# The RWKV-7 recurrence put on the crossing quadrants of TensorE, and run in common beats with the inversion and the scores

## The reference, cut to what matters

```python
def wkv7(r, w, k, v, a, b):
    # S_t = S_{t-1} diag(w_t) + (S_{t-1} a_t) b_t^T + v_t k_t^T ;  y_t = S_t r_t
    def step(S, inp):
        r_t, w_t, k_t, v_t, a_t, b_t = inp
        sa = jnp.einsum('bhvk,bhk->bhv', S, a_t)
        S = S * w_t[:, :, None, :] + sa[..., None] * b_t[:, :, None, :] + v_t[..., None] * k_t[:, :, None, :]
        y = jnp.einsum('bhvk,bhk->bhv', S, r_t)
        return S, y
```

## Time and profile before

| | us |
|---|---|
| median of 3 executions | 2024.97 |
| the profiled execution's own time | 2027.18 |
| its span, first to last instruction | 2025.4 |
| in it the stage of the change (L2182 to the start of L2347) | 213.5 |

### The profile page before, as it was taken

The page is one execution under the profiler, slowest core; times in us unless marked ns, Lnnn a source line. Parts: engine busy times, 40 slices in busy tenths (PEclk is TensorE's granted clock), DMA queues, the critical chain, the costliest instruction groups (busy, mean ns, idle before and its releaser), DMA issues.

```text
span 2025.4 us, 35146 instructions
## 1 busy us (share of the span) xinstructions
PE 1967.9 (97%) x14308; PEld 1602.1 (79%) x14308; DVE 1158.7 (57%) x1805; ACT 783.1 (39%) x1399; POOL 207.3 (10%) x164
## 2 busy tenths in 40 slices
PE   7999999999999999998999999999999999999997
PEld 3877899877787887775777887877888888888885
DVE  6789666576434444466475747485555256556423
ACT  7767333334222222437532222134243244344211
POOL 2000222200202012004202102020000010000001
PEclk9999999999999999998999999999999989999999
DMA  5320000222333222220244454534531222332421
GB/s 194 138 94 22 3 4 4 86 102 82 102 101 94 93 94 84 90 89 32 91 161 159 153 171 141 191 141 144 171 104 32 65 92 83 106 101 83 148 92 42
DMA packets 61004, 201.48 MB, mean 99 GB/s; under 512 B 8000, under 2 KB 11200, under 8 KB 59584
## 3 DMA queue, kind: packets, MB, share of 16 engines
q1 hardware_dynamic: 60096, 192.93, 28.7%
q10 hardware_dynamic: 768, 6.55, 1.0%
HBM read 190.68 MB, written 6.42 MB: 97 GB/s over the span
## 4 chain that ended last, share of the span: by engine, by line
PE 71%; issue 17%; DVE 7%; ACT 2%; POOL 2%; DMA 0%; DVEq 0%; POOLq 0%; SPq 0%; ACTq 0%
PE bank L2033 17%; PE bank L2035 17%; PE bank L2034 17%; POOL HS L2843 2%; PE bank L2218 1%; PE bank L2250 1%; PE bank L2265 1%; PE bank L2222 1%; DVE GBZ L1435 1%; DVE HR L1618 1%; PE bank L2519 1%; DVE wlo L1251 1%; PE bank L2505 1%; PE bank L2539 1%; PE bank L2682 1%
## 5 line engine op out<-in xcount | busy, mean ns | idle before, releaser
L1251 DVE TENSOR_TENSOR wlo<-raw,whi 128x1024 fp32r<-128x1024 f32 x270 | 327.3, 1222 | 568.9 <-ACT whi L696 566.3
L696 ACT ACTIVATE whi<-raw 128x1024 fp32r<-128x1024 f32 x270 | 282.3, 1057 | 708.6 <-PE bank L2035 695.7
L2033 PE MATMUL bank<-inh,whi 128*128 128x512 f32 x1200 | 470.7, 392 | 1.9 <-DVE inl L1495 1.6
L2035 PE MATMUL bank<-inh,wlo 128*128 128x512 f32 x1200 | 467.1, 389 | 0.0
L2034 PE MATMUL bank<-inl,whi 128*128 128x512 f32 x1200 | 467.0, 389 | 0.0
L2033 PEld LDWEIGHTS bank<-inh,whi 128*128 128x128 f32 x1200 | 225.2, 188 | 58.3 <-issue 6.6
L2035 PEld LDWEIGHTS bank<-inh,wlo 128*128 128x128 f32 x1200 | 225.2, 188 | 47.1
L2034 PEld LDWEIGHTS bank<-inl,whi 128*128 128x128 f32 x1200 | 225.3, 188 | 46.8 <-issue 0.7
L2033 PE MATMUL bank<-hidh,whi 128*128 128x512 f32 x576 | 228.5, 397 | 8.2 <-DVE HR L1618 5.5
L2035 PE MATMUL bank<-hidh,wlo 128*128 128x512 f32 x576 | 224.5, 390 | 0.0
L2034 PE MATMUL bank<-hidl,whi 128*128 128x512 f32 x576 | 224.3, 389 | 0.0
(11 more groups left out here) (423 smaller groups left out, 2853.0 us busy)
## 6 DMA issues: line engine op xcount, KB each, us to landing
raw<-in_mlp_w SPq DMA_DIRECT2D x128, 512.0 KB, 3.6
ADW<-in_w_ada SPq DMA_DIRECT2D x32, 768.0 KB, 5.0
raw<-in_w_up SPq DMA_DIRECT2D x44, 512.0 KB, 3.5
raw<-in_w_in SPq DMA_DIRECT2D x28, 512.0 KB, 3.7
raw<-in_a_w_rkv SPq DMA_DIRECT2D x24, 512.0 KB, 3.5
raw<-in_w_down SPq DMA_DIRECT2D x22, 512.0 KB, 3.5
raw<-in_a_wo SPq DMA_DIRECT2D x8, 512.0 KB, 7.6
raw<-in_b_wq SPq DMA_DIRECT2D x8, 512.0 KB, 3.4
```

The source lines that it names most:

```text
L696: act.activation(whi[u % SLOTS][:, :], raw[u % SLOTS][:, :], ACT.Copy).then_inc(w_hi, 1)
L1251: dve.tensor_tensor(lo[:, :], r[:, :], h[:, :].bitcast(F32), ALU.subtract).then_inc(w_lo, 1)
L2033: pe.matmul(o, w[:, wc], xh, start=start, stop=False)
L2035: return pe.matmul(o, r[:, wc], xh, start=False, stop=stop)
```

## The change

The token space of a head moves to the other partition half. The scores of head h are still read from `head(h)` but are written to `head(1 - h)` (`cross(h)`), which is the quadrant off the diagonal. VT, KT, BT, the masked scores, the inverse, WB and UB of head h so lie on the other half. The state and the channels stay. By this the narrow and wide scores, the product A S (`correction`, bank 4) and the four products into bank 6 (`off`) are crossing matmuls; the inversion and the products into bank 5 (`output_states`, `values_sum`, `solved`) stay on the diagonal.

The three loops are replaced by one over 50 beats. Ten beats make one pair of chunks, two beats (one for each chunk) a level. A beat of TensorE has three slots: the left product of one chunk, interleaved matmul by matmul with `off` of the recurrence or with a narrow score job; the bank 5 products with a narrow score job; the right product of the left product of the beat before, with a wide score job. Then comes `correction`, and in the first eight beats one bonus sum each. The pair in the inversion is g, the recurrence runs on g-1 in steps of two blocks (8 steps in 10 beats), the scores belong to g and g+1. What a job's table does not have for the last pair is left out there. The last ten beats hold the recurrence of the last pair alone.

The recurrence is arranged anew: ScalarE copies the three products of bank 5 at once (128x384); VectorE adds the A S part and the values part into WB, adds the two parts of the output into RT, and makes the new state in two instructions of 128x64; GpSimd multiplies AT and RT of each chunk but the first by the decay FS (`scaled`, two 128x512 instructions), which the state is no longer multiplied by beforehand. ScalarE squares a whole chunk of the output at once. Z and the inverse have two banks (0 and 1) in place of four. GBZ has six buffers in place of four. `early_sums` runs in beat 42, the three early reciprocals in beats 44 to 46. SyncE waits for `off` of step 23 (beat 39) and of step 31 (beat 49).

The number of matmuls does not change: 768 in the scores, 1280 in the inversion, 992 in the recurrence, 8 bonus and 8 early sums, 3056 in all.

```diff
+        GROUPS = NCH // 2
+        PER, RPER = 2 * LEVELS, CB
+        BEATS = PER * GROUPS + RPER + 2
+        MASKED = {0: (0, 3), 1: (0, 4), 2: (2, 0), 4: (2, 1), 5: (1, 3), 7: (1, 4), 8: (3, 0), 9: (3, 1)}
+        COPIED = {0: (0, 5), 1: (2, 2), 3: (0, 6), 4: (0, 7), 6: (1, 5), 7: (3, 2), 8: (1, 6), 9: (1, 7)}
+        AHEAD_OF_TIME = (((0, 0), 2), ((0, 1), 4), ((0, 2), 3), ((1, 0), 6), ((1, 1), 7), ((1, 2), 5))
+        VSUM_AT, VROOT_AT, VINV_AT = PER * GROUPS + 2, PER * GROUPS + 3, (PER * GROUPS + 4, PER * GROUPS + 5, PER * GROUPS + 6)
+
...
+        GBZ = [at(f"GBZ{n}", kb, [CB, P]) for n, kb in enumerate((32, 40, 192, 196, 16, 24))]
...
-            sp.wait_ge(STEP["pe_rec"].sem, STEP["pe_rec"].at(("y", NCH // 2 - 2, 2 * CB - 1)))
+            sp.wait_ge(STEP["pe_rec"].sem, STEP["pe_rec"].at(("off", RPER * (GROUPS - 1) - 1)))
...
+            for beat in range(BEATS + 1):
+                q, u, c, r = inverse_at(beat), recurrence_at(beat - 1), job_at(COPIED, beat), recurrence_at(beat - 3)
+                w2 = recurrence_at(beat + 1)
+                if q:
+                    act.wait_ge(pi.sem, pi.at(("q", *q)))
+                    act.activation(QS[q[2]][:], pairs(PB[q[2]][:]), ACT.Copy).then_inc(ai.sem, ai.step(("q", *q)))
+                if u is not None or w2 is not None:
+                    part = slice(2 * P if u is None else 0, 2 * P if w2 is None else 3 * P)
+                    act.wait_ge(pr.sem, pr.at(("diag", beat)))
+                    act.activation(DIAG[beat % 2][:, part], PB[5][:, part], ACT.Copy).then_inc(ar.sem, ar.step(("diag", beat)))
+                if c:
+                    score_copy(*c, 3)
+                if r is not None and r % (RPER // 2) == RPER // 2 - 1:
+                    j = chunk_of(r)[0]
+                    act.wait_ge(dr.sem, dr.at(("y", r)))
+                    act.activation(KT[:, :, tok(j)], RT[:, :, tok(j)], ACT.Square).then_inc(ar.sem, ar.step(("y", j)))
+                if beat == VROOT_AT:
+                    act.wait_ge(STEP["pe_gn"].sem, STEP["pe_gn"].at("early"))
+                    act.activation(KNI[:, 0:EARLY], PB[0][:, 0:EARLY], ACT.Sqrt, scale=1.0 / HD, bias=small[:, 1:2]).then_inc(ag.sem, ag.step("early root"))
...
+            def states_next(r):
+
+                j, cbs = chunk_of(r)
+                dve.wait_ge(pr.sem, pr.at(("off", r)))
+                if j > 0:
+                    dve.wait_ge(dr.sem, dr.at(("m", r - RPER // 2)))
+                for n in range(2):
+                    cb = cbs.start + n
+                    if j == 0:
+                        mm = dve.tensor_copy(SM[1][:, cb, :], PB[6][:, tok(n)])
+                    else:
+                        mm = dve.scalar_tensor_tensor(SM[(j + 1) % 2][:, cb, :], SM[j % 2][:, cb, :], FS[:, cb, j - 1:j], PB[6][:, tok(n)], ALU.mult, ALU.add)
...
+            for beat in range(BEATS):
+                z, m, w, y = inverse_at(beat - 1), job_at(MASKED, beat), recurrence_at(beat), recurrence_at(beat - 2)
+                if y is not None:
+                    if y < RPER * GROUPS - RPER // 2:
+                        states_next(y)
+                    outputs(y)
+                if z:
+                    inverse_sum(*z)
+                if m:
+                    score_mask(*m, 2)
+                if w is not None:
+                    corrections(w)
+                if beat == 0:
+                    turned(0, 0, 1)
+                if z:
+                    g, lv, x = z
+                    if lv < LEVELS - 1:
+                        turned(g, lv + 1, x)
+                    elif g < GROUPS - 1:
+                        turned(g + 1, 0, x)
+                if beat < CB:
+                    bonus(beat)
+                if beat in VINV_AT:
+                    early_inverse(VINV_AT.index(beat))
             dve.drain().then_inc(phase, 1)
             dve.wait_ge(phase, phase_done("dve"))
             pg, ag = STEP["pe_gn"], STEP["act_gn"]
@@ -2176,171 +2236,215 @@
 
             dsc, atk = STEP["dve_score"], STEP["act_tok"]
             din, ain, drc, arc = STEP["dve_inv"], STEP["act_inv"], STEP["dve_rec"], STEP["act_rec"]
...
+            def score_wide(j, job, bank, a):
+
+                cb = a + 4 * (job % 3)
+                for h in range(2):
+                    hs = head(h)
+                    mm = pe.matmul(PB[bank][cross(h), chunk(a)], (BT if job < 2 else KT)[hs, cb, tok(j)], RA[hs, :, cb, tok(j)], start=True, stop=True)
+                if a == 3:
...
+            def off(r, n):
+
+                j, cbs = chunk_of(r)
+                cb, part = cbs.start + n // 4, n % 4
+                if part < 2 and j < NCH - 1:
+                    for h in range(2):
+                        ts = cross(h)
+                        if part == 0:
+                            pe.matmul(PB[6][head(h), tok(n // 4)], KT[ts, cb, tok(j)], VT[j % 4][ts, cb, :], start=True, stop=False)
                         else:
+                            pe.matmul(PB[6][head(h), tok(n // 4)], BT[ts, cb, tok(j)], UB[(beat_of(r) + 1) % 2][ts, tok(n // 4)], start=False, stop=True)
+                if part >= 2:
+                    for h in range(2):
+                        ts = cross(h)
+                        if part == 2:
+                            mm = pe.matmul(PB[6][head(h), tok(2 + n // 4)], VT[j % 4][ts, cb, :], GKM[j % 4][ts, cb, 0:HC], start=True, stop=False)
                         else:
+                            mm = pe.matmul(PB[6][head(h), tok(2 + n // 4)], UB[(beat_of(r) + 1) % 2][ts, tok(n // 4)], GBZ[j % 6][ts, cb, 0:HC], start=False, stop=True)
+                    if n == 7:
+                        mm.then_inc(pr.sem, pr.step(("off", r)))
...
+                    mm = pe.matmul(PB[5][head(h), tok(n)], GBZ[j % 6][head(h), cb, HC:P], WB[r % 2][head(h), tok(n)], start=True, stop=True)
...
+                for n in range(2):
+                    cb = cbs.start + n
+                    for h in range(2):
+                        mm = pe.matmul(PB[4][cross(h), tok(n)], AT[head(h), cb, tok(j)], SM[j % 2][head(h), cb, :], start=True, stop=True)
+                mm.then_inc(pr.sem, pr.step(("w", r)))
...
+            for beat in range(BEATS):
+                q, z = inverse_at(beat), inverse_at(beat - 1)
+                m, c = job_at(MASKED, beat), job_at(COPIED, beat)
+                w, u, y, w2 = (recurrence_at(beat - ago) for ago in (0, 1, 2, -1))
+                c_at = 0 if y is None else 2 if m is None and z else 1
+                if c and c_at == 0:
+                    score_free(COPIED, beat)
+                if y is not None:
+                    off_ready(y)
+                if q:
+                    inverse_left_ready(*q)
+                for n in range(CB):
+                    if q:
+                        inverse_left(*q, n)
+                    if y is not None:
+                        off(y, n)
+                    elif c and c_at == 0:
+                        score_narrow(*c, 3, n)
+                if c and c_at == 1:
+                    score_free(COPIED, beat)
+                if w2 == 0:
+                    pe.wait_ge(dp.sem, dp.at(("bonus", CB - 1)))
+                elif u is not None or w2 is not None:
+                    pe.wait_ge(arc.sem, arc.at(("diag", beat - 1)))
+                for n in range(CB):
+                    if n in (0, 1) and w2 is not None:
+                        mm = values_sum(w2, n)
+                        if n == 1 and u is None:
+                            mm.then_inc(pr.sem, pr.step(("diag", beat)))
+                    if n in (2, 3) and u is not None:
+                        output_states(u, n - 2)
+                    if n in (4, 6) and u is not None:
+                        mm = solved(u, n // 2 - 2)
+                        if n == 6:
+                            mm.then_inc(pr.sem, pr.step(("diag", beat)))
+                    if c and c_at == 1:
+                        score_narrow(*c, 3, n)
+                if z:
+                    pe.wait_ge(ain.sem, ain.at(("q", *z)))
+                    pe.wait_ge(din.sem, din.at(("t", *z)))
+                if m:
+                    score_free(MASKED, beat)
+                if c and c_at == 2:
+                    score_free(COPIED, beat)
+                for n in range(CB):
+                    if z:
+                        inverse_right(*z, n)
+                    if m and n % 2 == 0:
+                        score_wide(*m, 2, n // 2)
+                    if c and c_at == 2:
+                        score_narrow(*c, 3, n)
+                if w is not None:
+                    correction(w)
+                if beat < CB:
+                    bonus(beat)
+                if beat == VSUM_AT:
+                    early_sums()
...
+            for x in range(2):
+                prepare(x)
+                level_mask(0, 0, x)
+            for g in range(GROUPS):
+                for lv in range(1, LEVELS):
                     for x in range(2):
```

(37 more changed lines are left out.)

406 lines of the change are left out of this document (164 added, 242 removed).

## The result

| | before | after |
|---|---|---|
| median, runs | 2029.27 us, 7 | 2014.70 us, 7 |
| lowest to highest | 2024.61 to 2031.27 | 2010.99 to 2021.21 |
| ratio, 95% interval | | 0.9937 (0.9922 to 0.9952) |
| ratio on a second chip job (6 and 12 runs) | | 0.9936 (0.9924 to 0.9947) |
| the profiled execution: time, span | 2027.18, 2025.4 | 2010.99, 2009.0 |

0.9937 of 2029 us is 12.8 us less (9.7 to 15.8); forecast were 16. The profiled execution of after was the fastest of its seven, so its 16 us are at the upper end; a second trace, of a run of 2017.0 us span, has a stage of 200.9 us. Of the executions behind the experiments, one of 3239.92 us (mean granted clock 0.555; the kernel "both heads, apart") is left out of its ratio, and the trace of "both heads at once" is of its slowest execution, 2235.49 us, where the median is 2204.46.

The account below looks back on a forecast made before the run. TensorE's instruction supply, 256 per 3.80 us, was to bound the kernel: 170.7 us before the tail against 143 of work, then 22.2 + 3, ending the stage at 411.9 instead of 428.0; 2024.97 - 16 = 2009 us, range 1976 to 2028.

Parts of the forecast that it names:

- The matmul time: TensorE's beats without supply limits: four quadrants overlap fully, a beat takes 3.6 to 3.85 us, ten beats 36.6.
- rival 2: Slots with two kinds of work: crossing quadrants do not work beside diagonal ones; 2054 us, chance 0.12.
- rival 3: TensorE starts small matmuls no faster than a floor, 25 ns; a block takes 4.03 us, median 2020; chance 0.10.
- The supply: TensorE's instruction blocks before the tail: one per 3.80 us (3.7 to 4.0), 44.9 blocks, 170.7 us against 143 of work.
- rival 1: TensorE's instruction supply keeps up because blocks could be asked for earlier; 1977 us, chance 0.12.
- The z wait does not add to it: Left product's wait for VectorE's sum, 1.04 us a beat, costs nothing beyond the supply, wherever in a block it falls.
- The clock: TensorE's times were taken at granted clock 1.00, the 2.4 GHz level, with no term for a fall.
- The first pair: First ten beats, no recurrence: 2.9 us a beat by work; 228 records a beat, 3.5 us by supply.
- The tail: Beats 40 to 49, recurrence alone: starts at 386.7, lasts 22.2 us plus 3 (0 to 6) for SyncE's loads.
- The whole: Kernel time: 16 us less, from base 2024.97 to 2009 us; the profiled execution 2011.

Follow-up runs that it names:

- both heads, apart: Kernel "both heads at once" with its shared inversion matmuls in slots of their own, not alternating with 64-row ones; ratio 0.9877 to the kernel before.
- both heads at once: The changed kernel with inversion matmuls of the last three chunk pairs issued once for both heads (128 rows), computing something else; ratio 1.0847 to the kernel before.

## Why the prediction was right, step by step

- **The matmul time** was right. Four quadrants overlap in full, so rival 2 is out, and matmuls of a slot start 15 ns apart on average (four in 0.058 us), so there is no floor of 25 ns, rival 3. The floor of about 25 ns from start to start, which the Trainium skill states in "TensorE: Matmul & The Clock Gate" (section "Wait — 56ns, not 53.3ns?"), this trace does not show for matmuls of different quadrants. Beats 30 to 32 took 3.76, 3.65 and 3.83 us; forecast were 3.6 to 3.85. The one halt among them of more than 0.5 us, 1.0 us at 348.76, lies in the piece in which the left product waits for the sum anyway.
- **The supply** was right, and rival 1 is out: taking away 22 us of overlap cost no time that can be told from noise, taking away instructions gave 20 us once the early waits had gone too. Ten beats took 46.8 and 46.6 us (forecast 46 to 47), a block 3.85 and 3.95 (3.80, bounds 3.7 and 4.0), the stage 197.7 and 200.9 (197). The Trainium skill calls the crossing mostly hidden ("Runtime: NRT & Kernel Launch", section "Instruction fetch mechanics"). This case's trace disagrees: 33 of 35 crossings had a halt over 0.1 us, 25 us in all.
- **"The z wait does not add to it, since a block is asked for when the block before is entered, whatever waits inside it"** was wrong. A wait that falls early in the block, at instruction 11 to 71 in 35 of 35 cases, holds the next packet back: 5 blocks at 4.80 us beside 29 at 3.69. The mean is 3.85, so by luck the step's error was covered by a turnaround taken from the earlier trace rows that was 0.1 too long for an undisturbed block of that trace. In the second trace the 29 take 3.81, and nothing covers the 5 (4.81): the mean is 3.95.
- **The clock** was taken as full throughout. In the beats it fell three times to 1.2 GHz, for 3.4 us each (at 268.9, 316.7 and 384.9 us; granted clock 0.96 in each stretch of ten beats), each time 1.2 to 1.5 us after the end of a halt of 1.5 to 1.7 us; after others as long it did not. In the stage of before it had not fallen. That most of it costs nothing where the supply is the bound is argued, not shown; the second trace had two such falls in the beats and longer blocks.
- **The first pair** took 31.3 us for its ten beats, 28.2 forecast by work. The forecast's count of 228 instructions a beat was wrong: the trace has 203 and two waits or so, so the supply (31 us at 3.85 a block) and the work end almost together. A bonus sum takes 1.05 us and not 0.86, and the beats with one 3.05 to 3.23 in place of 2.95.
- **The tail**, from beat 40 on, began at 389.2 in place of 386.7 and lasted 23.4 in place of 25.2 us; of it the loads cost 3.4 to 3.8 in place of 3.
- **The whole**: 12.8 us in place of 16. The profiled execution, forecast at 2011, took 2010.99, but that it agrees to the tenth is luck: the seven executions spread over 10 us, and it is the fastest. The median is 2014.70 where 2009 was forecast. 4.3 us of these 5.7 come from the base, which was the median of three executions of before (2024.97; of seven it is 2029.27), and the rest from the smaller gain (14.6 us between the medians). The second trace has 3.3 us more in the stage: its blocks last 3.95 us, 0.05 of the added 0.10 in the packets' own length, and over 36 blocks that makes 3.6 us. Why packets take longer in one execution than in another is open.

## What to carry to other kernels

Count instructions, not only engine time. Here TensorE was supplied with 256 instructions in 3.8 to 4.0 us on average (67 a microsecond at 3.8). An fp32 matmul is four instructions. Small ones that start closer than 15 ns to the next instruction on average gain nothing, and packing quadrants stops paying there. Look for "issue" halts at equal distances in instructions, with one instruction packet in each. Once there, fewer instructions help, and shorter work does not. A wait that falls at instruction 11 to 71 of a block delayed the next packet each time and made its block 1.1 us longer, so look where the waits fall, and put work that is ready into them; how much of the 0.3 to 0.5% that this gave in time comes from the late packets is not shown.

## What the runs showed of the hardware that I had not expected

- Where every crossing halts, a block's turnaround has three parts: 1.3 us on average to the packet's start, 0.9 to 1.5 for its 16 KB, 1.4 to the first instruction. No two packets are under way at a time in any trace here; at least 2.2 us lie between the end of one and the start of the next.
- A change between 64-row and 128-row matmuls costs 0.15 us at full clock and 0.24 at half clock, in both directions; between quadrants of 64 rows no such gap shows.
- A stretch full of such changes ran at 1.2 GHz for 167 us on end although TensorE's busy row says 163 of 167. The row counts the gaps as busy: from 280 to 430 us there are 300 changes of 0.24 us, 73 us in which no matmul starts. Why the clock fell is not shown.
